# A paired u1 stage whose one-hot gate tiles are shared between VectorE and GpSimd

## What is computed

```python
act = jax.nn.gelu(jnp.einsum('thkd,td->thk', u[ib], tb), approximate=False)
return jnp.einsum('thk,thkd->td', gb * act, v[ib])
```

## Time and profile before

| what | value |
|---|---|
| median of 3 executions | 3020.26 us (3019.74 to 3021.7) |
| profiled execution | 3021.33 us |
| its span | 3019.3 us, 49593 instructions |
| TensorE matmuls busy | 2982.0 us (99%) |
| TensorE weight loads busy | 2793.4 us (93%) |
| VectorE busy | 2251.8 us (75%) |
| ScalarE busy | 1393.3 us (46%) |
| GpSimd busy | 187.8 us (6%) |
| granted clock of TensorE | 0.998 of full speed |

### The profile page before, as it was taken

How to read it: one execution, slowest core, us unless ns; L and a number is a source line. 1 busy time by engine, 2 the same in 40 slices (tenths; PEclk the granted TensorE clock), 3 DMA queues, 4 the chain that set the end, 5 groups by cost and what they waited for, 6 DMA issues and landing times.

```text
span 3019.3 us, 49593 instructions
## 1 busy us (share of the span) xinstructions
PE 2982.0 (99%) x19430; PEld 2793.4 (93%) x19430; DVE 2251.8 (75%) x3296; ACT 1393.3 (46%) x1494; POOL 187.8 (6%) x233
## 2 busy tenths in 40 slices
PE   8999999999999999999999999999999999999998
PEld 8899889999999999999999999999788888888887
DVE  5777659999868888888988877788656646565564
ACT  4464354466435454545454555444444333333333
POOL 1000000020001111111111000000000000000000
PEclk9999999999999999999999999999999999999999
DMA  5433454567768999999999874544444555555554
GB/s 211 180 141 140 154 202 176 191 227 254 242 255 309 362 352 367 354 352 350 352 355 355 324 272 168 197 168 158 164 167 167 193 190 187 195 189 188 193 193 155
DMA packets 102148, 705.60 MB, mean 234 GB/s; under 512 B 13016, under 2 KB 13040, under 8 KB 18464
## 3 DMA queue, kind: packets, MB, share of 16 engines
q1 hardware_dynamic: 78272, 562.07, 50.7%
q0 software_dynamic: 21872, 128.10, 12.1%
q10 hardware_dynamic: 1872, 13.63, 1.1%
HBM read 685.46 MB, written 18.24 MB: 233 GB/s over the span
## 4 chain that ended last, share of the span: by engine, by line
PE 91%; DVE 6%; ACT 2%; issue 1%; DMA 0%; POOL 0%; POOLq 0%; DVEq 0%; ACTq 0%
PE bank L2071 30%; PE bank L2058 16%; PE bank L2036 7%; PE bank L2022 7%; PE bank L2037 7%; PE bank L2115 7%; PE bank L2099 7%; PE bank L2116 7%; DVE pick_a L1634 2%; DVE split L1161 1%; DVE pick_b L1629 1%; ACT split L718 1%; DVE raw_lo L1161 1%; PE bank L2184 1%; PE bank L2148 1%
## 5 line engine op out<-in xcount | busy, mean ns | idle before, releaser
L718 ACT ACTIVATE split<-raw 128x2048 fp32r<-128x2048 f32 x532 | 1018.2, 1914 | 935.1 <-PE bank L2071 382.6
L1161 DVE TENSOR_TENSOR raw_lo<-raw,split 128x2048 fp32r<-128x2048 f32 x292 | 668.6, 2290 | 384.8 <-ACT split L718 383.5
L2071 PE MATMUL bank<-a_both,split 128*128 128x416 f32 (+1 forms) x4096 | 892.4, 362 | 0.8 <-DVE split L1161 0.5
L2071 PEld LDWEIGHTS bank<-a_both,split 128*128 128x128 f32 x4096 | 749.3, 188 | 42.1 <-issue 0.9
L1161 DVE TENSOR_TENSOR split<-raw,split 128x2048 fp32r<-128x2048 f32 x240 | 549.0, 2288 | 56.4 <-ACT split L718 36.3
L2036 PE MATMUL bank<-a_both,split 128*128 128x256 f32 (+1 forms) x1984 | 488.0, 286 | 0.3 <-DVE a_both L1180 0.2
L2037 PE MATMUL bank<-a_both,split 128*128 128x256 f32 (+1 forms) x1984 | 478.0, 281 | 0.0
L2058 PE MATMUL bank<-a_both,split 128*128 128x208 f32 x3072 | 417.1, 271 | 0.0
L2058 PEld LDWEIGHTS bank<-a_both,split 128*128 128x128 f32 x3072 | 395.3, 191 | 0.2
L2036 PEld LDWEIGHTS bank<-a_both,split 128*128 128x128 f32 x1984 | 380.7, 192 | 4.7 <-issue 2.6
L2037 PEld LDWEIGHTS bank<-a_both,split 128*128 128x128 f32 x1984 | 381.0, 192 | 0.5
(11 more groups left out here) (346 smaller groups left out, 2583.0 us busy)
## 6 DMA issues: line engine op xcount, KB each, us to landing
raw<-stream_dram SPq DMA_DIRECT2D x532, 1024.0 KB, 4.8
gates_scratch<-stage ACTq DMA_DIRECT2D x13, 1024.0 KB, 4.3
gbuf<-gates_scratch POOLq DMA_DIRECT2D x30, 416.0 KB, 7.8
x<-x_dram SPq DMA_DIRECT2D x4, 512.0 KB, 6.5
x_scratch<-x POOLq DMA_DIRECT2D x1, 2048.0 KB, 11.4
mem<-mem_dram POOLq DMA_DIRECT2D x1, 2048.0 KB, 12.1
xm<-x_scratch POOLq DMA_DIRECT2D x1, 2048.0 KB, 13.6
out_dram<-x SPq DMA_DIRECT2D x4, 512.0 KB, 3.0
```

Source lines behind the costliest of these rows:

```text
L718: eng.activation(high(k, is_near(k))[:, :], raw[:, k % RAW, :], ACT.Copy).then_inc(hi_done, 1)
L1161: eng.tensor_tensor(low(k, is_near(k)), raw[:, k % RAW, :], high(k, is_near(k))[:, :].bitcast(F32), ALU.subtract).then_inc(split_done, 1)
L2071: last = mm(o, hi[:, kt * P:kt * P + P], tile(kt), start=kt == 0, stop=False, skip_group_check=True)
```

## The change

u1's units become paired. ScalarE copies the half with the first part to `act1` (`act1_half`), VectorE adds the other half from the bank (`add_half1`, two units later), and ScalarE applies Gelu in place and frees the bank (`gelu1`, two units later).

For groups whose place in the unit is 0, 2 or 4 (`SCALED_BY_POOL`), VectorE makes the four first-side tiles as one 128x512 comparison without the gates (`places_done`), and GpSimd multiplies each of the four by its gates in place (`oha_scaled`); TensorE waits for that. For the other groups nothing changes but the counts. The tiles lie in three sets, so `picks(q)` waits for q - 3.

On GpSimd the multiplies stand ahead of all else in this stretch, and the 36 small loads now come behind the first two gate loads. VectorE waits once more for `bank_free` before e0's first unit, since Gelu now writes `act1` later.

```diff
-        pick_a = at("pick_a", [P, 8, P], F32, work_at + 24576)
-        pick_b = at("pick_b", [P, 8, P], F32, work_at + 28672)
+        pick_a = at("pick_a", [P, 12, P], F32, work_at + 23040)
+        pick_b = at("pick_b", [P, 12, P], F32, work_at + 29184)
...
+        SCALED_BY_POOL = [q for q in range(1, GROUPS) if (q + 2) % 5 in (0, 2, 4)]
+        POOL_NTH = {q: n for n, q in enumerate(SCALED_BY_POOL)}
+        DVE_NTH = {q: n for n, q in enumerate(q for q in range(GROUPS) if q not in POOL_NTH)}
...
# GpSimd, ahead of load_gates; the 36 loads behind idx_done move behind load_gates(0, 3)
+            for n, q in enumerate(SCALED_BY_POOL):
+                eng.wait_ge(places_done, n + 1)
+                for i in range(4):
+                    one, t = pick_a[:, 4 * (q % 3) + i, :], G + 4 * q + i
+                    eng.tensor_scalar(one, one, pickT[:, 2, t:t + 1], None, ALU.mult).then_inc(oha_scaled, 1)
...
# ScalarE
+            def gelu1(k):
+                eng.wait_ge(act1_sum, k + 1)
+                eng.activation(act1[:, k, 0:TD], act1[:, k, 0:TD], ACT.Gelu).then_inc(bank_free, 1)
...
                 eng.wait_ge(mm_done, u + 1)
-                eng.activation(act1[:, k, 0:TD], bank[k % 4][:, 0:TD], ACT.Gelu).then_inc(bank_free, 1)
+                eng.activation(act1[:, k, 0:TD], bank[k % 4][:, TD:2 * TD], ACT.Copy).then_inc(act1_half, 1)
                 ahead_near(u)
+                if k >= 2:
+                    gelu1(k - 2)
                 for q in groups[4:]:
                     evict_group(q)
+            gelu1(14)
+            gelu1(15)
...
# VectorE
-                if q >= 2:
-                    eng.wait_ge(g_mm, 4 * (q - 1))
-                j = 4 * (q % 2)
+                if q >= 3:
+                    eng.wait_ge(g_mm, 4 * (q - 2))
+                j = 4 * (q % 3)
...
+                if q in POOL_NTH:
+                    eng.tensor_tensor(pick_a[:, j:j + 4, :], iota4, pickT[:, 0, ts].unsqueeze(2).to_broadcast([P, 4, P]),
+                                      ALU.is_equal).then_inc(places_done, 1)
+                    return
...
+            def add_half1(k):
+                eng.wait_ge(act1_half, k + 1)
+                eng.tensor_tensor(act1[:, k, 0:TD], act1[:, k, 0:TD], bank[k % 4][:, 0:TD], ALU.add).then_inc(act1_sum, 1)
...
                         ahead(UNIT0["u1"] + k - 1)
+                        if k >= 2:
+                            add_half1(k - 2)
...
             for k in range(LAST_GROUP, 16):
                 ahead(u1 + k)
+                add_half1(k - 1)
...
+            add_half1(15)
+            eng.wait_ge(bank_free, 4 * ROUND0["e0"] + 4)
...
# TensorE
-                    eng.wait_ge(oha_done, 4 * q + i + 1)
-                    j = 4 * (q % 2) + i
+                    if q in POOL_NTH:
+                        eng.wait_ge(oha_scaled, 4 * POOL_NTH[q] + i + 1)
+                    else:
+                        eng.wait_ge(oha_done, 4 * DVE_NTH[q] + i + 1)
+                    j = 4 * (q % 3) + i
...
-                feature_unit(k, UNIT0["u1"] + k + 1, a1, between=between, c0=G, near=True)
+                part_unit(k, UNIT0["u1"] + k + 1, a1_both, between=between, c0=G)
```

More of the change, by code:

```diff
@@ L365, in build @@
         oha_done = sem("oha_done")
+        places_done = sem("places_done")
+        oha_scaled = sem("oha_scaled")
+        act1_half = sem("act1_half")
+        act1_sum = sem("act1_sum")
         ohb_done = sem("ohb_done")
@@ L651, in _ @@
             load_gates(0, 3)
+            eng.wait_ge(idx_done, 1)
+            for i, (t0, n) in enumerate(SETS):
+                ts = slice(t0, t0 + n)
+                for c in range(P // n):
+                    ps, js = slice(c * n, c * n + n), slice(c * n, c * n + n)
+                    eng.dma_start(row_idx[ps, ts], pick_idx[ts, js]).then_inc(s_idx, 16)
+                    eng.dma_start(row_gate[ps, ts], picked[ts, 0, 2, js]).then_inc(s_idx, 16)
+                    eng.dma_start(row_rs[ps, i:i + 1], stat[ts, 2:3]).then_inc(s_idx, 16)
             for r in range(1, 3):
@@ L1624, in picks @@
             def picks(q):
-                if q >= 2:
-                    eng.wait_ge(g_mm, 4 * (q - 1))
-                j = 4 * (q % 2)
-                eng.tensor_tensor(pick_b[:, j:j + 4, :], C("iota").unsqueeze(1).to_broadcast([P, 4, P]),
-                                  pickT[:, 1, G + 4 * q:G + 4 * q + 4].unsqueeze(2).to_broadcast([P, 4, P]),
+                if q >= 3:
+                    eng.wait_ge(g_mm, 4 * (q - 2))
+                j = 4 * (q % 3)
+                iota4 = C("iota").unsqueeze(1).to_broadcast([P, 4, P])
+                ts = slice(G + 4 * q, G + 4 * q + 4)
+                eng.tensor_tensor(pick_b[:, j:j + 4, :], iota4, pickT[:, 1, ts].unsqueeze(2).to_broadcast([P, 4, P]),
                                   ALU.is_equal).then_inc(ohb_done, 1)
+                if q in POOL_NTH:
+                    eng.tensor_tensor(pick_a[:, j:j + 4, :], iota4, pickT[:, 0, ts].unsqueeze(2).to_broadcast([P, 4, P]),
+                                      ALU.is_equal).then_inc(places_done, 1)
+                    return
                 for i in range(4):
```

8 lines of the change are left out of this document (removed).

## The result

The changed kernel takes 3072.99 us (median; 3071.79 to 3073.2) where the kernel before takes 3020.53. The ratio is 1.0171, with a 95% interval of 1.0159 to 1.0183. I had forecast 3013.3 us and a range that ended at 3034. The direction was wrong, and the size was outside the range.

What follows compares the result with a forecast made beforehand. VectorE was taken to bound u1's gate-making units at 10.35 us each. Terms -12.9 + 2.6 + 0.4 + 3.0 = -6.9 us took the profiled 3021.33 to 3014.4; the median, 1.1 lower, was forecast at 3013.3, range 3008.5 to 3034.

Steps and rivals of the forecast that it cites:

- Masks, adds and TensorE's unit: In u1, masks for 30 groups save 12.9 us, nine VectorE adds cost 2.6; TensorE's five-group unit takes 9.0 us.
- the price of 9.9 / 120 = 0.08 us for a multiply: Mean cost to the chain per GpSimd multiply above which the prediction decided for slower.
- The multiply's price: One GpSimd multiply of a 128x128 tile in u1 was taken as 0.30 us for its two operands.
- GpSimd's own speed is not the limit: In u1, twelve GpSimd multiplies a unit were 3.6 us of a 9.4 us unit.
- the sum by engines: While u1 makes groups, VectorE's 9.4 us a unit limits; TensorE's 9.0 and ScalarE's near 8.3 lie under it.
- ScalarE costs nothing, its cover is only 1 us: ScalarE's half copy and separate Gelu in u1 add about 0.3 us, reaching near 8.3 of 9.4: no cost.
- Interference: GpSimd and VectorE in u1: 3 to 4 meetings a unit of some 0.08 us, +3.0 us over ten units.
- The lock-out rival: GpSimd multiplies get no turn beside VectorE in u1, TensorE then VectorE wait: 11.4 us a unit, 3031.1 us; chance 0.29.
- The tail: Units 11 to 15: VectorE's turns of 5.60 us limit, so nothing is gained and 0.4 us lost.
- The moved queue: GpSimd's 36 small loads behind the gate loads cost nothing; rival: 5 to 10 us late, 3016.3 us, chance 0.07.
- the sum without interference: Rival: u1's multiplies find room and meetings cost nothing, -12.9 + 2.6 + 0.4 = -9.9, 3010.3 us; chance 0.14.

Runs made afterwards that it cites:

- e10: Changed kernel with each GpSimd multiply replaced by a MEMSET (those groups' places and gates left out) and ScalarE's high part made earlier: 3017.02 us, ratio 0.9987.
- e1: Changed kernel with all groups' first-side tiles made by VectorE, no GpSimd multiply; pairing, three sets and moved loads stay: 3024.72 us, ratio 1.0013.
- e5: Changed kernel with each GpSimd multiply replaced by a MEMSET of the same tile (those groups' places and gates left out): 3026.94 us, ratio 1.002.
- e12: Changed kernel with all tiles made by VectorE, no GpSimd multiply, and ScalarE's high part made before the unit's end: 3026.12 us, ratio 1.0018.
- e16: Changed kernel with ScalarE's high part made before the unit's end and eight extra TensorE products a unit at place 2: 3055.87 us, ratio 1.0112.
- e13: Changed kernel with eight extra TensorE products a unit, ahead of the waits for GpSimd at place 2: 3053.19 us, ratio 1.0109.
- e14: Changed kernel with GpSimd multiplying only at place 2, plus eight extra TensorE products a unit there: 3049.79 us, ratio 1.0095.
- e6: Changed kernel with one GpSimd TENSOR_TENSOR of 128x512 a group, gates broadcast, instead of four multiplies: 3042.2 us, ratio 1.007.

## Why the prediction was wrong, by its own steps

**Masks, adds and TensorE's unit: right.** The unit of VectorE that I summed (9.4) is measured as 9.35 in e10, and 10.62 in e1 is the old 10.35 with the add. One slip of reading: the price of 9.9 / 120 = 0.08 us for a multiply is where the gain is used up, not where the kernel becomes slower.

**The multiply's price: wrong, 0.60 us for 0.30.** I took a TENSOR_SCALAR of two elements and added the slope of a MEMSET. A MEMSET of this very tile takes 0.20 us, the multiply 0.60. A MEMSET reads nothing and couldn't bound what reading costs. I gave an upper end only for being held up, none for the operation itself, though I named it last as what would break the forecast. Twelve a unit were 7.2 us unblocked and 9.4 as measured, not 3.6.

**"GpSimd's own speed is not the limit", and the sum by engines: the step that failed.** I compared each engine's work in a unit (9.4, 9.0, 8.3, 3.6) and took the largest. That holds only where work can be shifted freely between units. Here ScalarE's high part waited for the unit's end, and VectorE's split, the hand-over, the multiplies and TensorE's rest came one after the other. With the durations of the chain above: 1.9 + 2.3 + 0.3 + 1.2 + 3.4 is 9.1 us, and 5.6 more go by until the next high part (TensorE's remaining products, ScalarE's copies), 14.7 of the 14.8 measured. In the kernel before the same ring existed, with no GpSimd in it, and was shorter than VectorE's 10.35: its VectorE waited for a high part only once in u1, as its timeline shows. The prediction read the chain from 618.5 us on as VectorE alone and passed over that wait.

```profile
625.99 2.29 DVE L1161 TENSOR_TENSOR split<-raw,split 128x2048 fp32r<-128x2048 f32 x1 [0.39 <-ACT split L718]
```

**"ScalarE costs nothing, its cover is only 1 us": wrong.** Even at 0.20 us a multiply, VectorE waited 1.1 to 1.5 us a unit for the high part (e5), and opening that wait gave 9.9 us (e10 against e5), nothing where VectorE was full (e12 against e1), and nothing where GpSimd was slow (e16 against e13, though not at an equal clock).

**TensorE's clock: not in the sum at all.** My rows had 1.00 throughout, and I priced no stretch at another level. With TensorE waiting 2 to 3.5 us once a unit, it fell to 0.50 behind the wait, and the ring ran through the slow products. The extra work of e13 and e14 shows 20 and 16 us of this.

**Interference: right in size for VectorE, for a wrong reason, and left out for GpSimd.** A `pick_a` group took 1.23 us for 1.11, a mask 0.77 for 0.69, some 0.1 where they met, inside my 0 to 0.15. But VectorE's freedom was no rule of the chip: under operations of 512 elements its `pick_a` was held, 0.7 to 1.5 us a group. The other direction I had read rightly from the earlier trace rows and then given no price, since GpSimd had room: on the chain the four multiplies were held for 3.43 - 2.40 = 1.03 us.

**The lock-out rival: right in direction, small in size.** It had the path (GpSimd, TensorE in order, three full sets, VectorE waiting), and 28.6 us of VectorE's waits for TensorE in after are that. It gave 11.4 us a unit, not 14.6 to 15.9, because it counted 3.6 us of multiplies and left out the high part and the clock. Even its upper end, 3047, rested on multiplies of 0.30.

**The tail: right but for 0.8 us.** Splits 12 to 15 start at 783.02, 788.63, 794.23 and 799.84, 5.60 apart as summed, and the tail lost 1.2 us for a forecast of 0.4. **The moved queue: right**; gated1 waits for no late load.

Put together, the 52.5 us are: 6.4 that stay when a multiply costs 0.20 us (e5 over the kernel before), 20 to 24 of lowered clock (e13), and the remaining 22 to 26 that the dearer multiplies take through the rings at full clock. Between these 6.4 and the gain of 9.9 that the sum without interference had lie 16.3 us. The ring over the high part is 9.9 of them (e10 against e5); of the rest about 1 us lies in the tail, and the remainder wasn't taken apart. Of the 22 to 26 us, some ten may be multiplies that VectorE held up at place 2, an estimate from the 1.03 us of one unit times ten; no run isolates it. How the others divide between the first ring and that of the sets stays open, since opening one uncovers the other.

## What to carry to other kernels

Comparing the work of each engine per unit bounds the time from below only; before handing part of one tile's work to a third engine, follow one unit around through every engine until it comes back to its start, and sum that ring with each wait in it. The hand-over was dear right behind the step that all wait for (place 2, 41 us) and cheaper where its ring had two units to go round (place 4, 8 us). And a price for an operation that no row shows needs an upper end of several times the guess, above all if the nearest rows don't read what it reads.

## What the runs showed of the hardware

- GpSimd, 128 partitions, f32, shortest times: TENSOR_SCALAR of 128 elements with a scalar per partition 0.59 us, MEMSET of the same tile 0.20, TENSOR_SCALAR of 512 by a constant 1.49. From the last and the first, (1.49 - 0.59) / 384 is 2.3 ns an element and leaves some 0.3 us for each instruction, an estimate that takes a constant and a scalar per partition as equally dear. Comparison and multiply in one instruction of 128: a shortest time of 0.78 us, and a mean of 1.23 to 1.36 in use.
- Two neighbours hold each other up in both directions: a GpSimd multiply of 0.60 us took up to 2.19, and four VectorE TENSOR_SCALAR of 1.11 us in all took up to 2.57 beside GpSimd operations of 512 elements (e6), while three VectorE TENSOR_TENSOR in a row, with two SBUF inputs each, kept their 0.68 us and GpSimd's operation was the one held (2.63 us).
- TensorE's granted clock went to 0.50 for 2.3 us after it had been busy 1.57 of 3.47 us, and 20 us of a kernel's time came back when otherwise useless products filled that gap. Filling a wait with work made the kernel faster. The Trainium skill, page "TensorE: Matmul & The Clock Gate", section "What's actually happening", has the two levels, 1.2 and 2.4 GHz. This trace agrees: its stretches show 0.50 and 1.00, and the same group of products took 1.75 us in the changed kernel and 0.91 in e13.
